# Attention of a two-layer diffusion block: values held stationary, two heads in the two column halves of TensorE, the output divided on its way out of PSUM, and context heads scored in pairs

## What is computed

```python
def mla_attend(q_nope, q_rope, k_nope, k_rope, v):            # 8 heads, keys of 96, values of 64
    s = einsum('bqhd,bkhd->bhqk', q_nope, k_nope) + einsum('bqhd,bkd->bhqk', q_rope, k_rope)
    p = softmax(s * MLA_SCALE, axis=-1)
    return einsum('bhqk,bkhd->bqhd', p, v)

# windowed branch: 8 query heads, 2 key heads of 64, band of +-128 tokens, all context keys, one sink logit per head
p = softmax(concatenate([s_band, s_ctx, s_sink], axis=-1))
out = p[band] @ v_band + p[ctx] @ v_ctx
```

## Time and profile before

| | us |
|---|---|
| median of 3 runs | 3486.64 (3484.65 to 3489.26) |
| the profiled execution | 3490.27 |
| its span | 3488.5 |
| PE busy in the span | 3265.5 (94%) |
| DVE busy | 1749.9 (50%) |
| ACT busy | 1349.1 (39%) |
| branch m, layer 0: first S to last yT | about 189.6 to 345 |
| branch s, layer 0 | about 448.5 to 564.5 |
| branch m, layer 1 | about 2116.3 to 2230 |
| branch s, layer 1 | about 2309.8 to 2394.7 |

### The profile page before, as it was taken

How to read it: one execution, slowest core, us unless ns; L and a number is a source line. 1 busy time by engine, 2 the same in 40 slices (tenths; PEclk the granted TensorE clock), 3 DMA queues, 4 the chain that set the end, 5 groups by cost and what they waited for, 6 DMA issues and landing times.

```text
span 3488.5 us, 47535 instructions
## 1 busy us (share of the span) xinstructions
PE 3265.5 (94%) x14784; PEld 2344.6 (67%) x14784; DVE 1749.9 (50%) x2421; ACT 1349.1 (39%) x1901; POOL 611.8 (18%) x751
## 2 busy tenths in 40 slices
PE   7989999999998999999999599999999899999995
PEld 3468877799754676666766246877774567777662
DVE  1344143122264676667676524343334577776665
ACT  2244143122131555555554124333222355555551
POOL 0000120000033232232322000020001333333220
PEclk9989999999999999999999899999999999999998
DMA  6310211344402999999997820011331599999985
GB/s 227 109 61 7 73 32 64 99 139 138 170 32 110 339 381 363 364 372 380 371 378 283 340 51 24 31 40 55 91 120 53 224 376 367 364 370 358 346 323 241
DMA packets 222803, 720.79 MB, mean 207 GB/s; under 512 B 55650, under 2 KB 104196, under 8 KB 163396
## 3 DMA queue, kind: packets, MB, share of 16 engines
q1 hardware_dynamic: 177508, 626.97, 48.6%
q0 software_dynamic: 45184, 92.28, 7.2%
HBM read 701.35 MB, written 84.13 MB: 225 GB/s over the span
## 4 chain that ended last, share of the span: by engine, by line
PE 72%; DMA 15%; DVE 5%; issue 3%; ACT 3%; SPq 1%; POOLq 0%; DVEq 0%; POOL 0%; ACTq 0%
PE ps L749 11%; PE ps L751 11%; PE ps L750 11%; PE ps L818 7%; PE ps L742 7%; DMA ring<-in_w_exp_up 6%; PE ps L771 5%; PE ps L926 5%; PE ps L945 4%; PE ps L1019 4%; DMA region_v<-in_w_exp_up 3%; DMA ring<-y_rows 2%; DMA region_k<-in_w_exp_up 2%; PE ps L1038 2%; PE ps L846 1%
## 5 line engine op out<-in xcount | busy, mean ns | idle before, releaser
L771 PEld LDWEIGHTS ps<-con,region_c 128*128 128x128 f32 x1958 | 265.2, 169 | 140.5 <-issue 101.0
L1862 POOL DMA_INDIRECT y_rows<-region_q,idx_out x141 | 177.4, 1258 | 876.3 <-DVE region_q L1480 856.3
L771 PE MATMUL ps<-con,region_c 128*128 128x128 f32 x1958 | 291.7, 277 | 30.9 <-DVE region_c L1644 7.2
L751 PE MATMUL ps<-region_x_split,ring_split 128*128 128x384 f32 (+2 forms) x800 | 284.9, 356 | 0.0
L1099 ACT ACTIVATE region_q<-ps 128x512 f32<-128x512 f32 (+2 forms) x157 | 99.9, 636 | 390.5 <-PE ps L818 325.6
L749 PE MATMUL ps<-ring_split,region_q_split 128*128 128x512 f32 x568 | 230.5, 406 | 13.5 <-DVE ring_split L1446 13.1
L749 PE MATMUL ps<-region_h_split,region_q_split 128*128 128x512 f32 x560 | 225.8, 403 | 12.8 <-DVE ring_split L1446 12.7
L751 PE MATMUL ps<-ring_split 128*128 128x512 f32 x568 | 224.5, 395 | 0.0
L751 PE MATMUL ps<-region_h_split,ring_split 128*128 128x512 f32 x560 | 220.6, 394 | 0.0
L1272 ACT ACTIVATE region_c<-ps 128x768 f32<-128x768 f32 (+1 forms) x48 | 33.8, 705 | 414.0 <-PE ps L751 414.0
L1446 DVE TENSOR_TENSOR ring_split<-ps,region_q_split 128x1024 fp32r<-128x1024 f32 x141 | 171.8, 1219 | 7.6 <-ACT region_q_split L1099 7.5
(11 more groups left out here) (307 smaller groups left out, 7063.6 us busy)
## 6 DMA issues: line engine op xcount, KB each, us to landing
ring<-in_w_mod SPq DMA_DIRECT2D x24, 2048.0 KB, 8.0
region_k<-in_w_exp_gate SPq DMA_DIRECT2D x48, 1024.0 KB, 7.5
region_k<-in_w_exp_up SPq DMA_DIRECT2D x48, 1024.0 KB, 16.4
region_k<-in_w_exp_down SPq DMA_DIRECT2D x48, 1024.0 KB, 14.6
ring<-in_w_exp_gate SPq DMA_DIRECT2D x47, 1024.0 KB, 7.4
ring<-in_w_exp_up SPq DMA_DIRECT2D x47, 1024.0 KB, 16.7
ring<-in_w_exp_down SPq DMA_DIRECT2D x47, 1024.0 KB, 15.1
region_v<-in_w_exp_gate SPq DMA_DIRECT2D x46, 1024.0 KB, 7.3
```

The costliest lines, as they stand in the source:

```text
L751: last = mm(o, wl, xh, start=False, stop=k == len(stationary) - 1)
L771: last = nc.tensor.transpose(ps[0:t.shape[1], at:at + t.shape[0]], t, ident[0:t.shape[0], 0:t.shape[0]])
L1862: pool.indirect_dma_start(Y8, bass.IndirectOffsetOnAxis(ap=idx_out[:, s:s + 1], axis=0), yb[:, s, :], None, bounds_check=TOK * TOPK - 1, o ...
```

## The change

Items are now listed by `attention_items`. A context item is a tile and two heads, scored into one slot; a latent item is still a tile and one head. A PV covers two heads: of one context item, or of two latent items, and it stands behind the second of them. The order around it is changed too: PV(i-1) now comes right behind S(i+1) and ahead of T(i). In PV the values are the stationary operand (64 columns) and the turned probabilities move (128 columns); even heads write to partitions 0 to 63 and odd heads to 64 to 127 of the output bank, key tile by key tile in turn. The output is thus already turned. Job `rd` takes the place of yT: eight matmuls spread the reciprocals of the sums over the same layout, ACT copies them to `rows_d`, and the DVE part `y` multiplies the bank with them straight into `Y`. The drains keep their engines (even items DVE, odd items ACT), and the lists `HALF` and `split_now` keep their item numbers.

```diff
+def attention_items(l):
+    pairs = [(t, (h, h + 1)) for t in active(l) if t < CT for h in range(0, HEADS, 2)]
+    return pairs + [(t, (h,)) for t in active(l) if t >= CT for h in range(HEADS)]
...
     def attention(l, br):
-        items = [(t, h) for t in active(l) for h in range(HEADS)]
-        late = []
+        items = attention_items(l)
+        ends = [i for i, (t, heads) in enumerate(items) if heads[-1] % 2]
+        spread, out_ = [], []
         add("S", l, br, 0, drain="act" if br == "m" else "dve")
-        for i in range(len(items) + 2):
+        for i in range(len(items) + 3):
             if l == 0 and i in {"m": (3, 10, 17), "s": (16, 32)}[br]:
                 more_modulation()
             if i + 1 < len(items):
                 add("S", l, br, i + 1, drain="act" if br == "m" else "dve")
+            if i - 1 in ends:
+                add("PV", l, br, i - 1)
+                if items[i - 1][1][-1] == HEADS - 1:
+                    spread.append(items[i - 1][0])
             if i < len(items):
                 add("T", l, br, i, drain="act" if i % 2 else "dve")
-            for t in late:
-                add("yT", l, br, t, drain="act")
-            late = []
-            if 1 <= i <= len(items):
-                add("PV", l, br, i - 1)
-                if items[i - 1][1] == HEADS - 1:
-                    late.append(items[i - 1][0])
+            for t in out_:
+                add("y", l, br, t)
+            out_, spread = spread, []
+            for t in out_:
+                add("rd", l, br, t, drain="act")
...
                 elif kind == "PV":
                     l, br, i = a
-                    t, h = attn(l, br, i)[:2]
                     g = tiles_done[0]
-                    after(pe, "T", l, br, i)
-                    if h == 0 and g >= 2:
+                    pair = value_blocks(l, br, i)
+                    for u in sorted({u for blocks in pair for _, _, u, _ in blocks}):
+                        after(pe, "T", l, br, u)
+                    if pair[0][0][0] == 0 and g >= 2:
                         pe.wait_ge(o_drained, g - 1)
-                    ks = key_tiles(l, br, i)
-                    for j, kt in enumerate(ks):
-                        v = V[:, kt, VD * h:VD * h + VD] if br == "m" else VS[:, kt, HD * (h // 4):HD * (h // 4) + HD]
-                        last = mm(OB[g % 2][:, VD * h:VD * h + VD], PTb[:, i % 2, j * P:j * P + P], v,
-                                  start=j == 0, stop=j == len(ks) - 1)
+                    n = len(pair[0])
+                    for j in range(n):
+                        for blocks in pair:
+                            h, kt, u, at = blocks[j]
+                            v = V[:, kt, VD * h:VD * h + VD] if br == "m" else VS[:, kt, HD * (h // 4):HD * (h // 4) + HD]
+                            side, c = 64 * (h % 2), P * (h // 2)
+                            last = mm(OB[g % 2][side:side + 64, c:c + P], v, PTb[:, u % 2, at:at + P],
+                                      start=j == 0, stop=j == n - 1)
...
-                elif kind == "yT":
+                elif kind == "rd":
                     l, br, t = a
                     g = tile_no(l, br, t)
-                    pe.wait_ge(o_drained, g + 1)
-                    last = turn(ps, [(j * P, ytok[:, g % 2, j * P:j * P + P]) for j in range(4)])
+                    pe.wait_ge(rd_ready, g + 1)
+                    for h in range(HEADS):
+                        one = rden[:, 8 * (g % 2) + h:8 * (g % 2) + h + 1].broadcast_to([P, 64])
+                        side, at = 64 * (h % 2), P * (h // 2)
+                        last = mm(ps[side:side + 64, at:at + P], one, ident, start=True, stop=True)
...
                 elif kind == "S":
                     _, br, i = a
...
+                    for h, at, to, w in score_columns(l, br, i):
+                        p = Pb[:, i % 2, to:to + w]
+                        last = A_(p, ps[:, at:at + w] if br == "m" else p, ACT.Exp, scale=-1.0,
+                                  bias=nb[:, 8 * (g % 2) + h:8 * (g % 2) + h + 1], accum_out=den[:, 8 * (g % 2) + h:8 * (g % 2) + h + 1])
...
+                elif kind == "y":
+                    _, br, t = a
+                    g = tile_no(l, br, t)
+                    dve.wait_ge(o_full, g + 1)
+                    after(dve, "rd", l, br, t)
+                    tt(Y[br][:, :, t * P:t * P + P], OB[g % 2].rearrange("p (c n) -> p c n", c=4),
+                       rows_d[:, g % 2, :].rearrange("p (c n) -> p c n", c=4), ALU.mult).then_inc(o_drained, 1)
```

More of the change, by code:

```diff
@@ L905, in _ @@
                     l, br, i = a
-                    t, h, _, parts = attn(l, br, i)
+                    t, _, scored = attn(l, br, i)
                     if i == 0:
@@ L919, in _ @@
                             after(pe, "vs", l)
[L920 to L926, removed]
+                    for h, parts in scored:
+                        if br == "m":
+                            q = QT[0:96, h, t * P:t * P + P]
+                        else:
+                            q = QS[:, h // 2, t * P:t * P + P]
+                        for at, key, n in parts:
+                            k = KT[0:96, h, key:key + n] if br == "m" else KK[h // 4][h % 2][:, key:key + n]
+                            last = mm(ps[:, at:at + n], q, k, start=True, stop=True)
                 elif kind == "T":
@@ L932, in _ @@
                         pe.wait_ge(exp_ready, exp_no(l, i))
-                    n = len(key_tiles(l, br, i))
+                    n = sum(len(v) for v in key_tiles(l, br, i))
                     last = turn(ps, [(j * P, Pb[:, i % 2, j * P:j * P + P]) for j in range(n)])
@@ L993, in _ @@
                         if n2 == cc == 0:
-                            after(pe, "yT", l, "m", NT - 1)
+                            pe.wait_ge(o_drained, tile_no(l, "m", NT - 1) + 1)
                         last = project(ps, [w[:, k, cc * P:cc * P + P] for k in range(4)], [Ym[:, k, :] for k in range(4)],
@@ L1148, in weights_high @@
                 if i == 0:
-                    act.wait_ge(filled, names["yT", l, "s", NT - 1].fill)
+                    act.wait_ge(filled, names["rd", l, "s", NT - 1].fill)
+                elif i == 1:
+                    act.wait_ge(o_drained, tile_no(l, "s", NT - 1) + 1)
                 for k0, piece in gate_weights(i):
@@ L1225, in _ @@
                     _, br, i = a
-                    t, h, at, parts = attn(l, br, i)
-                    w = sum(n for _, _, n in parts)
+                    t = attn(l, br, i)[0]
                     g = tile_no(l, br, t)
@@ L1243, in _ @@
                 elif kind == "T" and mine:
-                    n = P * len(key_tiles(l, a[1], a[2]))
+                    n = P * sum(len(v) for v in key_tiles(l, a[1], a[2]))
                     last = copy(PTb[:, a[2] % 2, 0:n], ps[:, 0:n])
-                elif kind == "yT":
-                    t = a[2]
-                    last = copy(Y[a[1]][:, :, t * P:t * P + P], ps[:, 0:512].rearrange("p (c n) -> p c n", c=4))
+                elif kind == "rd":
+                    g = tile_no(l, a[1], a[2])
+                    if g >= 2:
+                        act.wait_ge(o_drained, g - 1)
+                    last = copy(rows_d[:, g % 2, :], ps[:, 0:512])
                 elif kind == "qs":
@@ L1608, in _ @@
                     _, br, i = a
-                    t, h, at, parts = attn(l, br, i)
-                    w = sum(n for _, _, n in parts)
-                    g = tile_no(l, br, t)
+                    t, heads, _ = attn(l, br, i)
+                    columns = score_columns(l, br, i)
+                    w, g = columns[0][3], tile_no(l, br, t)
                     dve.wait_ge(filled, job.fill)
-                    b1 = nb[:, 8 * (g % 2) + h:8 * (g % 2) + h + 1]
                     if br == "m":
-                        vec.tensor_reduce(b1, ps[:, 0:w], AX.X, ALU.min).then_inc(max_ready, 1)
+                        b0 = 8 * (g % 2) + heads[0]
+                        scored = ps[:, 0:w * len(heads)].rearrange("p (h n) -> p h n", h=len(heads)) if len(heads) > 1 else ps[:, 0:w]
+                        vec.tensor_reduce(nb[:, b0:b0 + len(heads)], scored, AX.X, ALU.min).then_inc(max_ready, 1)
                     else:
@@ L1631, in _ @@
                 elif kind == "T" and mine:
-                    n = P * len(key_tiles(l, a[1], a[2]))
+                    n = P * sum(len(v) for v in key_tiles(l, a[1], a[2]))
                     last = vec.tensor_copy(PTb[:, a[2] % 2, 0:n], ps[:, 0:n])
-                elif kind == "PV" and a[2] % HEADS == HEADS - 1:
+                elif kind == "PV" and last_head(l, a[2]):
                     _, br, i = a
```

73 lines of the change are left out of this document (43 added, 30 removed).

## The result

| | before | after |
|---|---|---|
| time, median (lowest to highest) | 3486.64 (3479.24 to 3489.26), 5 runs | 3514.86 (3510.88 to 3524.47), 5 runs |
| ratio, 95% interval | | 1.0084 [1.0066, 1.0102] |
| the profiled execution, its span | 3490.27, 3488.5 | 3514.86, 3512.9 |
| branch m, layer 0: first S to last PV | 153.3 | 156.8 |
| branch s, layer 0 | 113.6 | 118.4 |

The change is slower by 28.2 us by the medians, where 14.2 was forecast. In the profiled executions it is 24.4 us, made of +36.0 in the four attention stretches and -11.6 outside them. The part outside has to be read with care: over all the kernels of this study, whose edits hardly touch it, it lay between 3006 and 3036 us.

The account below looks back on a forecast made before the run. PE was taken to bound the attention stretches, hardly waiting in their latent parts. The terms -70.0 + 11.4 - 7.2 + 87 - 7 = +14.2 us gave 3501 us, range 3474 to 3524.

Parts of the forecast that it names:

- the term for the new waits (+87): All new waits of PE ahead of PV in the attention stretches, side work included: +87 us.
- PV, cheaper: PV in the attention stretches: two heads overlap in column halves, 53.5 ns a record instead of 107; -70.0 us with switching.
- The rival that the halves don't overlap: PV and rd records cost 107 ns each, 96 us more: 3597 us; chance 0.07.
- Entering and leaving: Switching PE into and out of the split array: 0.15 us a PV, 0.10 for latent pairs; bounds 0 and 0.34.
- rd for yT: At each tile's end, four transposes (0.44 us) go and eight matmuls (1.01 us) come: +11.4 us over 20 tiles.
- The multiply off PE's path, -7.2: The multiply by the sums no longer stands between PV and a PE job, so PE's wait goes: -7.2 us.
- The new wait: PE waits before PV for the odd T's copy on ACT: 1.0 us a latent pair in branch m.
- The value for 512 keys: PE's wait before PV for a branch s pair of 512 keys: estimated 1.0 us.
- What HALF and split items add: Extra wait for latent pairs beside side work: 1.2 us for HALF (14.4 in all), 0.73 for a weight split (8.8).
- My third rival: The clock falls in the new waits: 24 HALF and split pairs at 0.75, 21 us more, 3522 us; chance 0.10.
- Context pairs, -7: Pairing heads in the context tiles halves the round trips PE to DVE to ACT: -7 us, bounds 0 and -14.
- the signs that I named: Profile after: PV 1.3 to 1.45 us, waits before it about 1.0, 2.0 beside HALF, latent pair period 6.4 to 6.6.

Follow-up runs that it names:

- the run head by head: The changed kernel with each PV's matmuls issued for all key tiles of one head, then the other: 3590.76 us, ratio 1.0273 to the kernel before.
- HALF on odd heads: The changed kernel with HALF = 3, 5, ..., 17 in place of 2, 4, ..., 16: 3505.45 us, ratio 1.0024 to the kernel before.

## Where the prediction was right, and which of its steps failed

The direction and the mechanism were right: PE's work fell, and a new wait for the odd head's copy took more than was saved. The size was off, +28.2 us where +14.2 stood. Two steps failed: the term for the new waits (+87) was too small, with 1.0 to 1.1 us a pair where 1.14 to 1.27 were measured, some 11 us; and the clock was put at nothing in the sum, where it cost 10 us. Point by point:

- **PV, cheaper.** Right. Records start 54.7 ns apart (forecast 53.5). The rival that the halves don't overlap is out, by the run head by head.
- **Entering and leaving.** Forecast 0.15 us by modr, 0.10 for latent pairs, upper bound 0.34. Measured on an rd between a T and an S: 0.35. On a PV that waits, the entry is hidden, and what shows is 0.13 (1.46 to a T against 1.33 to an rd) and 0.05 on the T behind it (0.71 for 0.66). The bound that I put aside was the right number, and modr, between other kinds of work, a poor guide. The Trainium skill, "TensorEngine Tiling (Array Packing)", Key Properties, says that a change of tiling mode drains TensorE; the 0.35 us here agree that a change has a price. Taken over PV's 24 records it is 1.46 us against a forecast 1.39, 4 to 5 us over all pairs, and an S behind a T is 0.06 shorter than behind a PV, which gives about half of that back.
- **rd for yT.** Forecast +0.57 a tile; the periods say +0.73 on a plain pair. The job alone takes 1.02 us to the next start (297.33 to 298.35), as forecast (1.01); the rest is what it adds to the jobs around it (T 0.80 for 0.71, S 1.39 for 1.29). Beside side work a tile's end adds less, 0.99 (8.24 - 7.25) and 0.73 (8.46 - 7.73).
- **The multiply off PE's path, -7.2.** Right, but mostly outside the stretches. Before, PE stood 1.1 to 1.3 us ahead of the last yT of each stretch. Now rd follows the last PV at once:

```profile
344.47 1.53 PE L978 MATMUL ps<-region_c,region_v 128*64 128x128 f32 x24 [0.99 <-ACT region_c L1135]
345.80 1.07 PE L990 MATMUL ps<-con,rden 128*64 128x128 f32 x16
346.81 0.44 PE L777 MATMUL ps<-region_x_split,ring_split 128*128 128x384 f32 x1
```

- **The new wait, the first step that failed.** "PE waits 1.0 us for each latent pair", 1.1 and 1.0 in branch s. Measured 1.14, 1.27 and 1.25. The chain was exact (2.94 forecast, 2.95 measured). What I gave too small was the handover: under 0.1 us by the step from DVE to ACT, where from the end of a copy to PV's start it is 0.14; and I took S at 1.35, its cost behind a PV, where behind a T it is 1.29, so PE arrives earlier and waits longer (that part is no loss, as S gave it back). A plain pair of branch m adds up to 1.46 + 0.71 + 1.29 + 0.66 + 1.29 + 1.14 = 6.55, where the forecast had 1.39 + 0.65 + 1.35 + 0.65 + 1.35 + 1.0 = 6.39. The value for 512 keys was an estimate, "all terms shorter", and 0.25 too low. Over 32, 16 and 16 pairs this is 4.5 + 2.7 + 4.0 = 11 us, less the few that a modr covers. What HALF and split items add came out right: 7.73 - 6.56 = 1.17 (forecast 1.2) and 7.25 - 6.56 = 0.69 (0.73).
- **The clock, the second step that failed.** My third rival came true in part, beside the forecast. It had 24 pairs at 0.9 us each; it was seven pairs at 1.4, 10 us, five of them in layer 1. Five of the seven begin behind a wait of 2.15 us and one, beside a split, behind 1.67; the seventh comes right behind a modr. Where the waits are shorter (HALF on odd heads) layer 1's clock is 0.99. I gave this rival 0.10 as something in place of my sum, when it belonged in the sum as a term.
- **Context pairs, -7.** Up to the first latent PV, branch m of layer 0 took 51.5 us before and 42.3 after; less one modr (3.6) on the one side and one S more (1.35) on the other, that is 6.9 us gained, some 2 of them by the cheaper PV. The same reckoning for branch s (32.2 and 29.4) gives nothing. So -7 was, if anything, too much against the kernel before. Within the change the pairing is worth more: without it the kernel is 11.6 us slower. In the change's own trace the waits there did not halve, they moved: every second context PV waits 1.07 us, since PV now stands close behind its T there as well.

```profile
208.18 0.66 PE L978 MATMUL ps<-region_c,region_v 128*64 128x128 f32 x8 [1.07 <-ACT region_c L1135]
...
211.45 0.66 PE L978 MATMUL ps<-region_c,region_v 128*64 128x128 f32 x8
...
214.63 0.66 PE L978 MATMUL ps<-region_c,region_v 128*64 128x128 f32 x8 [1.07 <-ACT region_c L1135]
```

The account for the profiled executions: 14.2 forecast, about 12 from the pairs, 10 from the clock, 2 from rd; against it 9 outside the stretches (-11.6, where the forecast had about -2.5: four waits for the multiply, less four rd's). That gives 29, against the measured 24.4. The 5 us between them lie inside the stretches and are not placed one by one. The 9 us outside are not explained by any edit; they are well within what that part varied by from kernel to kernel. So the miss in the change's own parts was larger than the miss in the total, and that the total came out this near is in part luck.

Of the signs that I named, these held: PV at 1.46 us was just above 1.3 to 1.45; the wait released by ACT's copy, 0.98 us by the profile in the steady stretch and 2.15 beside HALF; a period of 6.56; PE's busy time down by 52; the context tiles of branch m faster by some 7. Layer 1's branch m was slower by 19.6 us, beyond the 8 to 14; the clock is 7 of them.

What stays open: why 11 of 54 pairs behind a wait of 1.6 to 1.75 us got the lower clock and the others of the same make did not, and why 3 of the 22 behind 2.15 us were spared. Between repeats of the same kernel it fell in part on different pairs.

## What to carry to other kernels

Before an engine's jobs are made shorter or put closer together, follow the chain of the operand that the next job reads (here minimum, exp, copy) and subtract what is left between the two on that engine; a saving of 1 us a pair turned into a wait of 1.1. Then ask which engine should do the last link: moving that one copy from the engine that has the exp ahead of it to the one that has only the minimum took the same change from 0.7 to 0.8% slower to 1.5% faster. Side work that stands inside that chain costs at least its own length (1.17 us for a HALF copy of 0.73 with its subtraction on DVE, 0.69 for a split of 0.53), and the HALF work cost nothing one item later.

## What the runs showed of the hardware

- Two column halves of PE overlap only if the instructions alternate between them: 24 records of 128 columns took 1.46 us alternating and 2.36 us one half after the other.
- Going into the split array and out again between full-array jobs cost 0.35 us, while between two split jobs in a row there was next to nothing (1.33 us from PV to rd, where 24 records at 54.7 ns are 1.31).
- An S took 1.35 us behind a PV of the kernel before, 1.29 behind a T and 1.39 behind an rd. The price of a job depends on its neighbour by several hundredths of a microsecond, and over some hundred jobs that is as much as the effect that was to be forecast.
- Within 1.4 us behind a wait of about 2.15 us, PE's granted clock fell from 1.00 to 0.50 in 19 of 22 pairs, behind 1.6 to 1.75 us in 11 of 54, behind 0.3 to 1.6 us in none of 65. In the change's trace such a pair took 1.2 to 1.6 us more.
